# Gate/up products of a hybrid decoder block from seven block products instead of eight, with weight sums made by adding transfers

## The reference

```
h = h + mixed @ w_out                       # end of the mixer part
f = rms_norm(h, ffn_norm)
gate, up = split(f @ w_gate_up, 2)          # (528 x 1024) @ (1024 x 5632), 2816 columns each
h = h + (silu(gate) * up) @ w_down          # (528 x 2816) @ (2816 x 1024)
```

## Time and profile before

| | |
|---|---|
| median of 3 runs | 1330.71 us (1330.43 to 1330.77) |
| span of the profiled execution | 1328.9 us |
| what the median has beyond that span | 1.8 us |
| PE busy | 1308.0 us, 98% of the span, 8670 matmuls |
| DVE, ACT, POOL busy | 646.2, 539.4, 543.9 us |
| bytes moved | 113.06 MB, mean 85 GB/s |

### The profile page before, as it was taken

The page is one execution under the profiler, slowest core; times in us unless marked ns, Lnnn a source line. Parts: engine busy times, 40 slices in busy tenths (PEclk is TensorE's granted clock), DMA queues, the critical chain, the costliest instruction groups (busy, mean ns, idle before and its releaser), DMA issues. The chain is left out here.

```text
span 1328.9 us, 22857 instructions
## 1 busy us (share of the span) xinstructions
PE 1308.0 (98%) x8670; PEld 1196.4 (90%) x8670; DVE 646.2 (49%) x1087; ACT 539.4 (41%) x874; POOL 543.9 (41%) x272
## 2 busy tenths in 40 slices
PE   7999999999999999999999999999999999999999
PEld 7989999999999999999998889988888888888887
DVE  4698888563333333322236998984633333331000
ACT  4575548533222222222235655485432222222221
POOL 3553313243443443444445553222444444444443
PEclk9999999999999999999999999999999999999999
DMA  5322110122222222232223221111222222223323
GB/s 186 93 68 69 60 49 33 45 100 96 84 90 95 83 90 95 84 106 95 95 83 107 71 74 55 48 33 39 98 87 94 94 95 95 95 95 97 108 95 126
DMA packets 33452, 113.06 MB, mean 85 GB/s; under 512 B 4337, under 2 KB 4977, under 8 KB 33393
## 3 DMA queue, kind: packets, MB, share of 16 engines
q1 hardware_dynamic: 32672, 111.18, 25.3%
q10 hardware_dynamic: 720, 1.09, 0.2%
HBM read 108.79 MB, written 2.10 MB: 83 GB/s over the span
## 5 line engine op out<-in xcount | busy, mean ns | idle before, releaser
L632 POOL TENSOR_TENSOR wlo<-raw,whi 128x1024 fp32r<-128x1024 f32 x200 | 490.0, 2451 | 722.0 <-ACT whi L1158 721.6
L1158 ACT ACTIVATE whi<-raw 128x1024 fp32r<-128x1024 f32 x200 | 211.9, 1059 | 582.3 <-PE ps L758 543.5
L752 PE MATMUL ps<-xhi,whi 128*128 128x264 f32 (+1 forms) x1096 | 327.6, 322 | 6.7 <-ACT whi L1158 6.7
L752 PE MATMUL ps<-xlo,whi 128*128 128x264 f32 (+1 forms) x1096 | 326.5, 321 | 0.0
L752 PEld LDWEIGHTS ps<-xhi,whi 128*128 128x128 f32 x1096 | 206.8, 189 | 23.8 <-ACT whi L1158 6.7
L752 PEld LDWEIGHTS ps<-xlo,whi 128*128 128x128 f32 x1096 | 206.7, 189 | 16.1
L758 PE MATMUL ps<-xhi,wlo 128*128 128x264 f32 (+1 forms) x1096 | 194.7, 321 | 0.1
L849 PE MATMUL ps<-xhi,whi 128*128 128x264 f32 (+1 forms) x632 | 178.2, 310 | 0.0
L758 PEld LDWEIGHTS ps<-xhi,wlo 128*128 128x128 f32 x1096 | 162.8, 188 | 16.5 <-issue 0.5
L850 PE MATMUL ps<-xlo,whi 128*128 128x264 f32 (+1 forms) x632 | 171.9, 300 | 0.0
L752 PE MATMUL ps<-hlo,whi 128*128 128x264 f32 (+1 forms) x528 | 157.3, 321 | 0.0
(11 more groups left out here) (209 smaller groups left out, 1717.5 us busy)
## 6 DMA issues: line engine op xcount, KB each, us to landing
raw<-in_weights SPq DMA_DIRECT2D x200, 512.0 KB, 3.4
out_hT<-h SPq DMA_DIRECT2D x7, 256.0 KB, 4.3
h<-in_hT SPq DMA_DIRECT2D x4, 264.0 KB, 6.3
h<-in_hT ACTq DMA_DIRECT2D x4, 264.0 KB, 5.8
cst<-in_consts SPq DMA_DIRECT2D x1, 780.5 KB, 9.3
xnb<-feat SPq DMA_DIRECT2D x20, 33.2 KB, 2.0
feat<-xnb SPq DMA_DIRECT2D x20, 33.2 KB, 2.0
cst<-in_consts SPq DMA_DIRECT2D x1, 532.0 KB, 4.4
```

What stands on the lines that cost most here:

```text
L632: nc.gpsimd.tensor_tensor(wlo[:, b], raw[:, b], whi[:, b].bitcast(F32), ALU.subtract).then_inc(split_done, 1)
L752: nc.tensor.matmul(bank(bank_no, cut.stop - cut.start), whi[:, b, k % KT], x(k)[t][:, cut], start=(first and k == ks[0] and t == 0), stop= ...
L1158: return nc.scalar.activation(whi[:, b], raw[:, b], ACT.Copy).then_inc(hi_done, 1)
```

## The change

Of the 22 gate/up column blocks of a layer the first is computed as before (units `U_GU` and `U_GU + 1`). The other 21 are now **groups**. A group takes gate and up weights of one column block, with odd and even row tiles, as a 2 x 2 block matrix (`B11`, `B12`, `B21`, `B22`, each 4 pairs of row tiles x 128 columns = 128 x 512 elements) and the tokens as two halves. Strassen's scheme in Winograd's form gives the block product from seven block products instead of eight (`PRODUCTS`), each 12 matmuls for 4 pairs: 84 matmuls with one token half (264 columns in the first layer, 256 in the last). Before, a column block took 96 matmuls of 264 columns in the first layer, or 48 of 512 in the last.

- **Tokens.** Four combinations of even and odd token tiles (`forms`, L2036 to L2046 of the changed program) are computed by DVE and split by ACT and DVE, beside the output projection.
- **Weights.** SP loads three raw blocks of a group (`load_group`, 768 KB) and puts B11 and B22 (512 KB) into the places of the sums P and V (`load_first_terms`). When they have landed, POOL issues two transfers with `accum_op=ADD` that add B21 from memory to both (256 KB each). DVE makes the other two sums R and T (`rt_sums`). ACT rounds (`raw_high`, `sums_high`), DVE subtracts (`raw_low`, `sums_low`). POOL makes no subtraction for groups.
- **Places.** There are two slots, for odd and even groups. The lows of the sums, `sums_lo`, lie in the place of the sums themselves (the sums are not kept), so a slot's sums can be loaded only when the PE has finished the products of the group two before. The even slot lies over `raw`, `whi` and `wlo`.
- **Results.** ACT copies two partial products out of PSUM (`snapshot`), DVE makes `u_sum`, `up_second`, `gates`, `up_first` and `hidden`. The seventh product is added up in the bank that `u_sum` reads, and waits for it. The norm factor is applied to the gate, but no longer to the up part; instead each down product is multiplied by it before it is added to `h` (two DVE operations for one).
- **Down.** The first two down units are interleaved by row range, so that they can start before all of `hhi` and `hlo` is there; the first 7 column blocks are rounded and subtracted in the 21st group, the others afterwards.

The core of the diff:

```diff
-N_PROJ, N_OUT, N_GU, N_DN = 24, KT, 2 * MF, 3 * KT
+N_PROJ, N_OUT, N_GU, N_DN = 24, KT, 2, 3 * KT
...
+PRODUCTS = ("a22_b22", "f1_v", "a21_b12", "f5_r", "f3_b11", "a11_t", "f4_p")
...
+            hi_b = sb("hi_b", [128, 7, BLOCK], F32R, even_groups)
+            with ExitStack() as before_low:
+                sums_b = sb("sums_b", [128, 4, BLOCK], F32, before_low)
+            sums_lo_b = sb("sums_lo_b", [128, 4, BLOCK], F32R, even_groups)
...
+                def load_group(n):
...
+                        sp.wait_ge(sv.group_lo, 3 * (g0 + n - 3) + 1)
+                    sp.dma_start(group_slot(n)[0].rearrange("p b n -> p (b n)"),
+                                 groups[l * GROUPS_7 + n - 1][:, STREAM_B11 * BLOCK:]).then_inc(sv.group_loaded[n % 2], 16)
+                def load_first_terms(n):
...
+                    elif n > 2:
+                        sp.wait_ge(sv.product_done, len(PRODUCTS) * (g0 + n - 2))
+                    sp.dma_start(group_slot(n)[2][:, SUM_P:SUM_V + 1].rearrange("p b n -> p (b n)"),
+                                 groups[l * GROUPS_7 + n - 1][:, STREAM_B11 * BLOCK:(STREAM_B22 + 1) * BLOCK]).then_inc(sv.pv_loaded[n % 2], 16)
...
+                for n in range(2, GROUPS_7 + 1):
+                    load_first_terms(n)
+                    if n < GROUPS_7:
+                        load_group(n + 1)
+                sp.wait_ge(sv.product_done, len(PRODUCTS) * (g0 + GROUPS_7 - 1))
...
+                for n in range(N_PROJ + 2, U_DN):
+                    split_unit(l * UNITS + n, n % 2)
+                for n in range(1, GROUPS_7 + 1):
+                    sums = group_slot(n)[2]
+                    pool.wait_ge(sv.pv_loaded[n % 2], 16 * loads_before(l, n))
+                    for a in (SUM_P, SUM_V):
+                        pool.dma_start(sums[:, a], groups[l * GROUPS_7 + n - 1][:, STREAM_B21 * BLOCK:(STREAM_B21 + 1) * BLOCK],
+                                       accum_op=ALU.add).then_inc(sv.pv_summed[n % 2], 16)
...
+                for n in range(1, GROUPS_7 + 1):
+                    _, hi, _, sums_lo, lo_raw = group_slot(n)
+                    at, seen = group_banks(n), 3 * (g0 + n - 1)
+                    if n == 2:
+                        pe.wait_ge(ev.acc_free, ACC_FFN)
+                    elif n > 2:
+                        pe.wait_ge(sv.gate_scaled, l * MF + n - 1)
+                    pe.wait_ge(sv.group_hi, seen + 1)
+                    rest = product(at["x"], hi[:, 1], lo_raw[:, 1], odd_tiles(t2), True)
+                    pe.wait_ge(sv.group_lo, seen + 1)
+                    low_products(at["x"], rest).then_inc(sv.product_done, 1)
+                    pe.wait_ge(sv.group_hi, seen + 2)
+                    rest = product(at["z"], hi[:, 3 + SUM_V], sums_lo[:, SUM_V], form(FORM_F1), True)
+                    pe.wait_ge(sv.group_lo, seen + 2)
+                    low_products(at["z"], rest).then_inc(sv.product_done, 1)
...
+                    pe.wait_ge(sv.group_hi, seen + 3)
+                    rest = product(at["y"], hi[:, 3 + SUM_R], sums_lo[:, SUM_R], form(FORM_F5), True)
+                    pe.wait_ge(sv.group_lo, seen + 3)
+                    low_products(at["y"], rest).then_inc(sv.product_done, 1)
...
+                    pe.wait_ge(sv.u_ready, g0 + n)
+                    rest = product(at["y"], hi[:, 3 + SUM_P], sums_lo[:, SUM_P], form(FORM_F4), False)
+                    low_products(at["y"], rest).then_inc(sv.product_done, 1)
...
+                pe.wait_ge(sv.gate_scaled, l * MF + GROUPS_7)
+                for s, kts in enumerate(DN_PARTS):
+                    k0 = sum(DN_PARTS[:s])
                     for b in range(2):
+                        for hf in range(len(parts)):
+                            unit_part(b, U_DN + 2 * s + b, 2 * b + hf, hf, parts, hidden_tiles, order=range(k0, k0 + kts),
+                                      first=(s == 0), last=(s == 2),
+                                      waits={k: [(sv.hid_ready, l * MF + k + 1)] for k in range(k0, k0 + kts)} if hf == 0 and b == 0 else {})
...
+                def raw_high(n):
+                    raw_blocks, hi, _, _, _ = group_slot(n)
+                    act.wait_ge(sv.group_loaded[n % 2], 16 * loads_before(l, n))
...
+                    elif n > 2:
+                        act.wait_ge(sv.product_done, len(PRODUCTS) * (g0 + n - 2))
+                    nc.scalar.activation(hi[:, 0:3], raw_blocks[:, RAW_B11:RAW_B12 + 1], ACT.Copy).then_inc(sv.group_hi, 1)
+                def sums_high(n):
+                    _, hi, sums, _, _ = group_slot(n)
+                    act.wait_ge(sv.pv_summed[n % 2], 32 * loads_before(l, n))
+                    nc.scalar.activation(hi[:, 3:5], sums[:, SUM_P:SUM_V + 1], ACT.Copy).then_inc(sv.group_hi, 1)
+                    act.wait_ge(sv.rt_summed, 2 * (g0 + n))
+                    nc.scalar.activation(hi[:, 5:7], sums[:, SUM_R:SUM_T + 1], ACT.Copy).then_inc(sv.group_hi, 1)
+                def snapshot(n, product, bank_name, to):
+                    act.wait_ge(sv.product_done, len(PRODUCTS) * (g0 + n - 1) + DONE[product])
+                    nc.scalar.activation(to, bank(group_banks(n)[bank_name], width), ACT.Copy).then_inc(sv.snapped, 1)
...
+                for n in range(1, GROUPS_7 + 1):
+                    if n < GROUPS_7:
+                        raw_high(n + 1)
+                    if n > 1:
+                        act.wait_ge(sv.gate_scaled, l * MF + n)
+                    snapshot(n, "a22_b22", "x", s0[:, 0:width])
+                    silu_gate(n - 1)
+                    if n > 2:
+                        act.wait_ge(sv.hidden, l * MF + n - 1)
+                    snapshot(n, "f1_v", "z", s1[:, n % 2, 0:width])
+                    if n < GROUPS_7:
+                        sums_high(n + 1)
...
+                def rt_sums(n):
+                    raw_blocks, _, sums, _, _ = group_slot(n)
+                    dve.wait_ge(sv.pv_summed[n % 2], 32 * loads_before(l, n))
+                    dve.wait_ge(sv.group_loaded[n % 2], 16 * loads_before(l, n))
+                    nc.vector.tensor_tensor(sums[:, SUM_R], sums[:, SUM_P], raw_blocks[:, RAW_B22], ALU.add).then_inc(sv.rt_summed, 1)
+                    dve.wait_ge(sv.rt_summed, 2 * (g0 + n) - 1)
+                    nc.vector.tensor_tensor(sums[:, SUM_T], sums[:, SUM_R], raw_blocks[:, RAW_B12], ALU.add).then_inc(sv.rt_summed, 1)
+                def raw_low(n):
+                    raw_blocks, hi, _, _, lo_raw = group_slot(n)
+                    dve.wait_ge(sv.group_hi, 3 * (g0 + n) - 2)
+                    nc.vector.tensor_tensor(lo_raw[:], raw_blocks[:, RAW_B11:RAW_B12 + 1], hi[:, 0:3].bitcast(F32),
+                                            ALU.subtract).then_inc(sv.group_lo, 1)
+                def sums_low(n, a, hi_count):
+                    _, hi, sums, sums_lo, _ = group_slot(n)
+                    dve.wait_ge(sv.group_hi, 3 * g0 + hi_count)
+                    nc.vector.tensor_tensor(sums_lo[:, a:a + 2], sums[:, a:a + 2], hi[:, 3 + a:5 + a].bitcast(F32),
+                                            ALU.subtract).then_inc(sv.group_lo, 1)
+                def u_sum(n):
+                    dve.wait_ge(sv.product_done, len(PRODUCTS) * (g0 + n - 1) + DONE["f5_r"])
+                    dve.wait_ge(sv.snapped, 2 * (g0 + n) - 1)
+                    nc.vector.tensor_tensor(u_part[:, 0:width], bank(group_banks(n)["y"], width), s0[:, 0:width], ALU.add).then_inc(sv.u_ready, 1)
...
+                def gates(n):
+                    at = group_banks(n)
+                    dve.wait_ge(sv.product_done, len(PRODUCTS) * (g0 + n - 1) + DONE["f4_p"])
+                    chain(nc.vector.tensor_tensor(w_part[:, 0:width], bank(at["y"], width), s0[:, 0:width], ALU.add))
+                    chain(nc.vector.tensor_tensor(bank(at["v"], width), bank(at["v"], width), w_part[:, 0:width], ALU.subtract))
+                    nc.vector.tensor_tensor(halves(sg[:, of]), two_banks(at["v"], width), halves(rstd[:, of]), ALU.mult).then_inc(sv.gate_scaled, 1)
+                def up_first(n):
+                    dve.wait_ge(sv.snapped, 2 * (g0 + n))
+                    chain(nc.vector.tensor_tensor(up[:, t1], w_part[:, 0:width], s1[:, n % 2, 0:width], ALU.subtract))
+                def hidden(n):
+                    dve.wait_ge(sv.sg_ready, l * MF + n + 1)
+                    nc.vector.tensor_tensor(hid[:, n, of], up[:, of], sg[:, of], ALU.mult).then_inc(sv.hidden, 1)
...
+                for n in range(1, GROUPS_7 + 1):
...
+                    else:
+                        gates(n - 1)
+                    if n < GROUPS_7:
+                        rt_sums(n + 1)
+                    if n > 1:
+                        up_first(n - 1)
+                        hidden(n - 1)
+                    if n < GROUPS_7:
+                        raw_low(n + 1)
+                    else:
+                        for k in range(EARLY_HID):
+                            hidden_low(k)
```

(41 more changed lines are left out.)

300 lines of the change are left out of this document (218 added, 82 removed).

## The result

The changed kernel takes **1610.9 us** (1610.5 to 1612.8, four runs) against 1330.7: ratio 1.2108, 95% interval 1.2091 to 1.2125. Forecast were 1455 us and a range of 1385 to 1560. The direction, the place and the chain were as forecast; the size was more than twice as large (+280 for +124), and the range missed it.

A forecast was written before the change was run, and what follows sets the result against it. The PE, busy for 98% of the span, was taken as the bound. Terms of 54 + 63 - 2 - 0.5 + 7.4 + 1.9 = +124 us on 1328.9, and 1.8 beyond the span, gave 1455 us; range 1385 to 1560.

The forecast's parts named there:

- the chain: In each group, load of P and V, adds, DVE up to u_sum, handovers and seventh product in series: 14.4 us.
- PE bound before, periods 11.7 and 11.15 us: Gate/up before the change: matmul number and pace set a column block's time, 11.7 us first layer, 11.15 last.
- a regular PE wait in each group, released by DVE's `u_part<-ps,s`, of about A: Sign of being right, in 304 to 600 us: the PE waits for DVE once a group, by about A.
- A: Time of a group's two adding transfers, put at 4.2 us, the middle between the estimates 3.4 and 4.9.
- some 6: Sign of being right: DVE idle before its sums, released by a transfer, for some 6 us a group.
- the ring: In groups, load, adds, DVE and seventh product, closed by DVE's order and the load's wait; forecast period 14.4 us.
- The 768 KB load behind it ... needs no one: On SP's queue behind the load of P and V: sent at once; that load was priced at 3.4 us.
- The clock as a rival with 9%: Clock falls to 1.2 GHz in each group's PE wait; seventh product 1.5 us longer, +60, 1515 us; chance 9%.
- DVE 4.7: DVE's operations in a group from its two sums up to u_sum(n) take 4.7 us in series.
- DVE as a bound: Rival in groups: DVE's 9.0 us of operations, slowed as beside POOL's subtraction, would not fit; no chance of its own.
- Entry to the down products, 2 x 3.7 us: After group 21 the PE waits 1.9 us for gates(21) and 1.8 for the eighth row tile; +7.4 us.
- The end: Last down products: four small DVE operations in series where a pair took 0.76 us; +1.1 us.

The follow-up runs named there:

- own_sums: Changed kernel with DVE making P and V from B21 loaded by SP, DVE's order by due time, two places for the copy s0: 1307.7 us.
- no_adds: Changed kernel without the adding transfers; DVE and ACT wait for the load of P and V alone: 1308.4 us.
- u_first: Changed kernel with DVE's u_sum(n) and up_second(n) ahead of the sums of group n+1, adds as they are: 1390.0 us.
- the four runs: Changed kernel with adds left out, copies from POOL, copies from SP, or both adds in one transfer: 1308.4, 1547.1, 1525.0, 1638.4 us.
- quiet: Changed kernel with the 768 KB load issued by SP only when the adds have landed: 1595.0 us.
- plain_adds: Changed kernel with the two adding transfers on POOL's queue replaced by copies, P and V being B21 alone: 1547.1 us.
- awake: Changed kernel with 40 further unread matmuls ahead of the seventh product in groups 2 to 20: 1559.5 us.
- own_sums_entry: As own_sums, with the seven hidden_low and ACT's roundings spread out in group 21, at the entry to the down products: 1301.7 us.

## Why the prediction was wrong, step by step

- **PE bound before, periods 11.7 and 11.15 us**: right. `own_sums` shows 84 matmuls at 10.25 and 9.93 us a group (loads at 342.67 and 506.67, 16 apart; 970.20 and 1119.13, 15 apart), as worked out.
- **The chain**: right in every link, and "a regular PE wait in each group, released by DVE's `u_part<-ps,s`, of about A" too: 5.8 us for an A of 6.1. Only A was not 4.2; with it DVE's wait before its sums came to 8.6 us ((181.8 + 172.3)/41) for "some 6", and the period to 18.3 for 14.4. `no_adds` (1308 us) and `u_first` (1390 us) show that it is the ring, not the work in it.
- **A = 4.2** ("I take the middle"): the step that failed first, by 1.9 us a group, 76 us in all. The bounds held it (1.8 to 8.9), the middle between 3.4 and 4.9 did not. The 3.4 assumed that the read of the destination is free; adding instead of copying costs 1.4. That this is near the 1.45 worked out from the earlier trace rows is luck: up to 0.7 of it is POOL's longer issue, which the forecast didn't have. But 4.9 too was short: it priced one larger transfer, where the four runs show a second one behind the first (4.65 with its issue and handover, for 3.4) and POOL's 0.6. The Trainium skill (DMA: Bandwidth & Descriptors, section on the anatomy of a GpSimd-issued DMA) gives about 2.0 us plus the bytes over 436 GB/s, from which I had estimated 3.2 us for A. Measured is 6.1, so the measurement decides against that estimate here.
- **"The 768 KB load behind it ... needs no one"**: wrong. It lies beside the load of P and V, which took 4.36 us instead of 3.4, and beside the adds. With the handover to POOL (0.28 for 0.12) the load's row in the table is 1.1 us over the forecast; `quiet` got 0.4 us a group back, in loads and adds together. The rest was not separated.
- **The clock as a rival with 9%, beside the forecast**: mis-sorted, the second step that failed; the sum has 1.6 us for the seventh product, and it took 3.03. The lower level isn't an alternative to the forecast's wait but came with it: in `plain_adds` the PE waits 166.2/40 = 4.2 us a group, just what the forecast had, and its seventh product takes 3.04 us too (405.06 to the next load at 408.10). The 0.51 at 413 us and `awake` (51 us) show what it cost. The evidence that I set against it, 1.27 us of work in 4 us at the start at clock 1.00, was one stretch and no repeated wait. The Trainium skill (TensorE: Matmul & The Clock Gate, section on HAM oscillation) says that waits between bursts of matmuls put the engine back to half rate; this case agrees, with 0.22 us a matmul instead of 0.12.
- **DVE 4.7**: 4.57. **DVE as a bound**: rightly given no chance; POOL computes nothing in the groups, and DVE's operations kept their lengths.
- **Entry to the down products, 2 x 3.7 us**: 3.39 and 1.79. The forecast set 1.7 us of matmuls against the wait for the eighth row tile in both layers; in the last one these 14 matmuls have 512 columns and take 14 x 0.2325 = 3.3 us, which is the difference. The PE's wait is for `gates(20)`, not `gates(21)`: `gate_scaled` counts the ordinary column block too. It begins the down products at 682.25, DVE `gates(21)` at 682.45, and then waits longer for the eighth row tile. The lower clock followed here too, 0.57 from 689 to 693 us, which the forecast did not have. **The end**: four small operations in series, 1604.67 to 1606.33 (1605.91 + 0.42), as forecast.

```profile
687.53 0.39 PE L874 MATMUL ps<-hhi,whi 128*128 128x264 f32 x1 [3.39 <-DVE hlo L2123]
```

The sum with what was measured: 18.33 and 18.28 for 14.4 and 14.3 add 20 x 3.93 + 20 x 3.98 = 158 us to 1455, the entry takes off 2.2: 1611 us. The period thus carries the whole miss; that the sum meets the time to the microsecond is in part luck, since the small terms (groups 1 and 21, the layer boundary, the clock behind the entry) were not measured one by one. The range failed because the misses have one sign and I had kept them apart: a dearer A and the dearer load lengthen the wait, and the clock follows from the wait. An A of 6 alone gives 1527 by the forecast's own rule, and with the clock's 60 it is 1587, above the range.

## What to carry to other kernels

When a step is put in series inside a loop, put what follows from its wait into the same case: here the lower clock behind it (3.0 us for 1.6) and the slower landing of what is sent meanwhile (4.2 us for 3.4). Look for where the ring closes before pricing its links: moving `u_sum` ahead of the sums was worth 221 us with the slow adds untouched, making the adds fast in the old order 264, and both together 303. A sum that an engine with time to spare makes in 1.2 us shouldn't be handed to transfers that take 6, least of all inside such a ring.

## What was not expected of the hardware

- An adding transfer of 256 KB from memory into a tile landed in 4.8 to 5.1 us, a copy on the same queue in 3.9. POOL spent 1.03 us on the issue of each add on average and 0.54 on that of a copy.
- The same copies from SP's queue landed in 3.8 to 3.9 us: the queue made no difference to the landing, only to what came before it.
- A destination of 512 KB with a repeated source, in one adding transfer, took 6.8 us, longer than two transfers of half the size (6.1 us together, both issues included).
- 40 matmuls a group that serve nothing, put into the PE's wait, made the kernel 51 us faster.
- DVE's lows at the entry took 8.75 us for seven where POOL's two subtractions ran beside them (`own_sums`, 524.57 to 533.32), and 4.42 us for seven in the changed kernel (675.87 to 680.29, POOL's from 680.07). `own_sums_entry` shows both in one place: three lows ahead of POOL's pair took 1.94 us, two beside it 5.61.
